# Twenty-eight of forty conditioning slabs move from the attentions to the feed-forward and from TensorE to VectorE

## What is computed

```python
silu_c = jax.nn.silu(c)
silu_cc = jax.nn.silu(c_ctx)
for layer in range(DEPTH):
    want_ctx = layer < DEPTH - 1
    mod = silu_c @ w_mod[layer] + b_mod[layer]      # 1024 -> 6 * 1024
    cmod = silu_cc @ w_mod[layer] + b_mod[layer]
    sh1, sc1, g1, sh2, sc2, g2 = jnp.split(mod[:, None, :], 6, axis=-1)
    ...
    hx = modulate(rms_norm(x, norm1_g[layer]), sh1, sc1)
    mx, mc = token_mixers(hx @ w_in[layer], ...)     # attentions, pooling, gates, projections
    x = x + g1 * mx
    hx = modulate(rms_norm(x, norm2_g[layer]), sh2, sc2)
    ...
    f = swiglu(h_all, ...) if layer % 2 == 0 else moe_swiglu(h_all, ...)
    ...
    x = x + g2 * fx
```

## Time and profile before

| | us |
|---|---|
| median of 3 runs | 2029.77 (2026.84 to 2030.6) |
| profiled execution | 2027.18 |
| its span, first to last instruction | 2025.4 |

### The profile page before, as it was taken

How to read it: one execution, slowest core, us unless ns; L and a number is a source line. 1 busy time by engine, 2 the same in 40 slices (tenths; PEclk the granted TensorE clock), 3 DMA queues, 4 the chain that set the end, 5 groups by cost and what they waited for, 6 DMA issues and landing times.

```text
span 2025.4 us, 48866 instructions
## 1 busy us (share of the span) xinstructions
PE 1977.5 (98%) x22688; PEld 1419.6 (70%) x22689; DVE 474.4 (23%) x974; ACT 458.3 (23%) x765; POOL 425.0 (21%) x145
## 2 busy tenths in 40 slices
PE   5999999999999999999999999999999999999997
PEld 3885788878888888876997566666666666666664
DVE  3246223220010101346543002111111102111112
ACT  4236522233212223436443000000000000000001
POOL 2400334446545445401550000000000000000000
PEclk8999999999999999999999999999999999999999
DMA  8338332231232323246467999999999999999990
GB/s 328 107 149 350 107 104 100 88 145 63 104 104 83 104 94 105 93 156 261 167 230 290 388 404 390 374 392 389 409 378 374 390 406 388 376 392 389 407 379 25
DMA packets 69856, 505.56 MB, mean 250 GB/s; under 512 B 7760, under 2 KB 7888, under 8 KB 9104
## 3 DMA queue, kind: packets, MB, share of 16 engines
q1 hardware_dynamic: 69264, 500.01, 64.0%
q0 software_dynamic: 384, 2.36, 0.3%
HBM read 501.29 MB, written 1.05 MB: 248 GB/s over the span
## 4 chain that ended last, share of the span: by engine, by line
PE 88%; POOL 3%; issue 3%; DMA 2%; ACT 1%; DVE 1%; SPq 0%; POOLq 0%; ACTq 0%; DVEq 0%
PE bank L1265 29%; PE bank L1277 14%; PE bank L811 12%; PE bank L812 12%; PE bank L813 12%; POOL w_lo L499 3%; DMA slab<-in_w_in 2%; PE bank L846 1%; PE turned L1040 1%; PE pv_bank L1058 1%; PE bank L1016 1%; DMA slab<-in_w_mod 1%; ACT H_NEW L1525 1%; PE bank L1251 0%; PE bank L1279 0%
## 5 line engine op out<-in xcount | busy, mean ns | idle before, releaser
L1265 PE MATMUL bank<-moe_slab,HE 128*32 128x256 f32 x10752 | 596.3, 379 | 1.3 <-DVE GT L2216 1.3
L1265 PEld LDWEIGHTS bank<-moe_slab,HE 128*32 128x32 f32 x10752 | 346.4, 110 | 231.4 <-DVE GT L2216 1.8
L499 POOL TENSOR_TENSOR w_lo<-slab,w_hi 128x2048 fp32r<-128x2048 f32 (+2 forms) x88 | 362.3, 4119 | 573.9 <-ACT w_hi L1484 573.8
L811 PE MATMUL bank<-H_HI,w_hi 128*128 128x512 f32 (+1 forms) x880 | 321.0, 365 | 4.7 <-POOL H_LO L724 3.6
L812 PE MATMUL bank<-H_LO,w_hi 128*128 128x512 f32 (+1 forms) x880 | 318.2, 362 | 0.0
L813 PE MATMUL bank<-H_HI,w_lo 128*128 128x512 f32 (+1 forms) x880 | 318.1, 361 | 0.0
L1277 PE MATMUL bank<-moe_slab,GE 128*32 128x256 f32 x4032 | 299.8, 379 | 0.0
L1279 PE MATMUL bank<-moe_slab,GE 128*32 128x256 f32 x1344 | 299.1, 379 | 0.0
L1277 PEld LDWEIGHTS bank<-moe_slab,GE 128*32 128x32 f32 x4032 | 165.8, 110 | 115.4
L1484 ACT ACTIVATE w_hi<-slab 128x2048 fp32r<-128x2048 f32 (+1 forms) x88 | 165.7, 1888 | 152.9 <-PE bank L813 145.5
L773 POOL TENSOR_TENSOR OUT<-OUT,RINVF 128x256 f32<-128x256 f32 x2 | 1.6, 814 | 946.4 <-DVE RINVF L2337 946.4
(11 more groups left out here) (229 smaller groups left out, 2032.6 us busy)
## 6 DMA issues: line engine op xcount, KB each, us to landing
moe_slab<-in_moe_up SPq DMA_DIRECT2D x224, 1024.0 KB, 7.4
moe_slab<-in_moe_w SPq DMA_DIRECT2D x112, 1024.0 KB, 7.2
slab<-in_w_in SPq DMA_DIRECT2D x38, 1024.0 KB, 4.9
slab<-in_ffn_w SPq DMA_DIRECT2D x30, 1024.0 KB, 4.8
slab<-in_w_mod SPq DMA_DIRECT2D x20, 1024.0 KB, 7.7
side_slab<-in_w_mod SPq DMA_DIRECT2D x20, 1024.0 KB, 9.1
start_slab<-in_w_mod SPq DMA_DIRECT2D x8, 1024.0 KB, 17.4
slab<-in_w_proj SPq DMA_DIRECT2D x8, 1024.0 KB, 4.9
```

What stands on the lines that cost most here:

```text
L499: engine.tensor_tensor(lo, raw, hi.bitcast(F32), ALU.subtract).then_inc(done, 1)
L811: mm(out, lhs[0], rhs[0], start=start, stop=False)
L1265: ins = mm(outs[t // 2][32 * b:32 * b + 32, 256 * (t % 2):256 * (t % 2) + 256], rows[t], w[:, 256 * b:256 * b + 256], start=first and t != ...
```

## The change

Units 10 to 23, 28 slabs, are no longer matmuls. Groups 0 to 4 (layer 0 without its last gate) stay with TensorE; six units and three turned groups run beside layer 0's attentions, in the first, third and fifth run of three steps, and none beside layer 1's.

The other seven groups come from `w_mod_rows`: the same weights transposed on the host, so that an output column lies on a partition and its 1024 weights along it. A row slab is 1 MB and holds two chunks of 128 columns. During layer 0's feed-forward VectorE multiplies each chunk by the conditioning row, which stands in every partition (COND_ROW, 1 MB, Silu on ScalarE), and sums it in the same instruction into its column of `MOD`. That is 80 instructions (48 for the 12 slabs that need both streams, 32 for the 16 that need one), placed by `mod_rows` after the HID multiplies and, in the first two parts, after each residual. Three more instructions add the biases.

SP loads COND_ROW once layer 0's second norm is through, and the row slabs into two buffers at fixed places of the ring's order (`ROW_LOADS`); from the third on each waits for the sums of the slab two before. The buffers lie on places that held BIAS, TMP and others, so layer 1's BIAS is loaded later, ahead of the slab `("in", 1, 2)`.

The diff without its context and its smaller edits (semaphores, the same conditions on the other engines):

```diff
-MOD_FIRST = (4, 16)
+MOD_FIRST = 4
 def mod_beside(layer, s):
-    return None if s % 3 == 2 else MOD_FIRST[layer] + 2 * (s // 3) + s % 3
+    q, i = divmod(s, 3)
+    return MOD_FIRST + q + i if layer == 0 and q % 2 == 0 and i < 2 else None
 def turned_beside(layer, s):
-    return MOD_FIRST[layer] // 2 + s // 3 if s % 3 == 2 else None
-OUT_OF_RING = [mod_beside(_l, _s) for _l in range(DEPTH) for _s in range(len(attention_steps(_l))) if _s % 3 == 1]
+    q, i = divmod(s, 3)
+    return (MOD_FIRST + q) // 2 if layer == 0 and q % 2 == 0 and i == 2 else None
+OUT_OF_RING = [mod_beside(0, _s) for _s in range(len(attention_steps(0))) if _s % 3 == 1 and mod_beside(0, _s)]
+MOD_GROUPS = 5
+ROW_SLABS = [(part, i) for part in range(MOD_GROUPS, 12) for i in range(4)]
+ROW_STREAMS = [2 if part <= 7 else 1 for part, _ in ROW_SLABS]
+def row_sums(r):
+    return 2 * sum(ROW_STREAMS[:r])
+ROW_LOADS = {4: 2, 7: 1, 9: 1, 11: 1, 13: 1, 14: 1, 15: 1, 16: 1, 17: 1, 19: 1, 21: 1, 23: 1, 25: 2, 26: 2, 27: 2,
+             28: 2, 29: 1, 30: 3, 32: 3}
+assert sum(ROW_LOADS.values()) == len(ROW_SLABS)
...
+        COND_ROW = at("COND_ROW", 164, [P, 2, D])
+        row_slab = [at(f"row_slab{i}", kb, [P, 2, D]) for i, kb in enumerate((172, 180))]
+        ROW_OUT = at("ROW_OUT", 148, [P, 2, D])
...
+            ffn_at = SLABS["w1", 0, 0]
+            row_at = iter(range(len(ROW_SLABS)))
+            def row_loads(n):
+                if n == 4:
+                    sp.wait_ge(h_lo_ready[0, 2], DC)
+                    sp.dma_start(COND_ROW[:].rearrange("p a n -> p (a n)"), a["cond_row"]).then_inc(cond_row_in, 16)
+                for _ in range(ROW_LOADS.get(n, 0)):
+                    r = next(row_at)
+                    if r >= 2:
+                        sp.wait_ge(rows_made, row_sums(r - 1))
+                    sp.dma_start(row_slab[r % 2][:].rearrange("p a n -> p (a n)"), a["w_mod_rows"][r])\
+                        .then_inc(row_in[r % 2], 16)
...
+                if order[n] == ("in", 1, 2):
+                    sp.wait_ge(rows_made, row_sums(len(ROW_SLABS)))
                     sp.dma_start(BIAS[:].rearrange("p a h n -> p (a h n)"), a["rel_bias"][1]).then_inc(bias_in[1], 16)
                 load_slab(n, order[n])
+                if n >= ffn_at:
+                    row_loads(n - ffn_at)
                 if order[n][0] == "mod" and order[n][1] % 2 == 0:
...
-                for i in OUT_OF_RING:
-                    if (i >= MOD_FIRST[1]) == layer:
+                if layer == 0:
+                    for i in OUT_OF_RING:
                         wait_mod(act, i)
...
+                        if before is None:
+                            act.wait_ge(cond_row_in, 16)
+                            af(COND_ROW[:], COND_ROW[:], ACT.Silu).then_inc(cond_row_ready, 1)
...
-                wait_taken(dve, ("turned_mod", 6 * layer + (1 if w == 1 else 4)))
                 part = 1 if w == 1 else 4
+                if 6 * layer + part < MOD_GROUPS:
+                    wait_taken(dve, ("turned_mod", 6 * layer + part))
+                else:
+                    dve.wait_ge(row_parts_made, 2 if w == 1 else 3)
+                streams = 1 if (layer, w) == (1, 2) else 2
                 lo = VEC_COLS[f"g{w}", layer][0]
...
+            row_of = iter([(r, m) for r in range(len(ROW_SLABS)) for m in range(2)])
+            def mod_rows(n):
+                for _ in range(n):
+                    r, m = next(row_of, (None, None))
+                    if r is None:
+                        return
+                    group, i = ROW_SLABS[r]
+                    layer, part = divmod(group, 6)
+                    streams = ROW_STREAMS[r]
+                    if m == 0:
+                        dve.wait_ge(row_in[r % 2], 16 * (r // 2 + 1))
+                    w = row_slab[r % 2][:, m, :]
+                    for n in range(streams):
+                        col = (part * DC + 2 * i + m) * 2 + n
+                        k = row_sums(r) + m * streams + n
+                        if k >= 2:
+                            dve.wait_ge(rows_made, k - 1)
+                        v.scalar_tensor_tensor(ROW_OUT[:, k % 2, :], w, 1.0, COND_ROW[:, n, :], ALU.mult, ALU.mult,
+                                               accum_out=MOD[layer][:, col:col + 1]).then_inc(rows_made, 1)
+                    if m == 0:
+                        continue
+                    if (group, i) in ((5, 3), (7, 3), (11, 3)):
+                        dve.wait_ge(rows_made, row_sums(r + 1))
+                        first = {5: 5, 7: 0, 11: 2}[group]
+                        chunks = DC * (part + 1 - first)
+                        made = MOD[layer][:, 16 * first:16 * (part + 1)].rearrange("p (c s) -> p c s", s=2)[:, :, 0:streams]
+                        lo = VEC_COLS["bmod", layer][0] + DC * first
+                        b = VEC[:, lo:lo + chunks].unsqueeze(2).to_broadcast([P, chunks, streams])
+                        v.tensor_tensor(made, made, b, ALU.add).then_inc(row_parts_made, 1)
             def feed_forward():
                 q = 0
+                dve.wait_ge(cond_row_ready, 1)
                 for part, n in enumerate(PART_CHUNKS):
                     for s in range(n // 2):
                         for m in range(2):
@@ -2121,7 +2209,17 @@
                             v.tensor_tensor(HID[:, q % 4, :], SILU[:, m, :], acc(k3)[:], ALU.mult)\
                                 .then_inc(freed(k3), 1)
                             q += 1
-                    residuals(0, 5, [("down", part, c // 2, c % 2) for c in range(DC)], (1, 1) if part == 2 else None)
+                            if m == 1 or part == 2:
+                                mod_rows(2 if m == 1 and part < 2 else 2 + 2 * m)
+                    if part == 0:
+                        dve.wait_ge(row_parts_made, 1)
+                    keys = [("down", part, c // 2, c % 2) for c in range(DC)]
+                    if part == 2:
+                        residuals(0, 5, keys, (1, 1))
+                        continue
+                    for c, key in enumerate(keys):
+                        residual(0, 5, key, c)
+                        mod_rows(1 + part)
...
-    a["w_mod"] = np.concatenate([slabs(w) for w in w_mod])
+    a["w_mod"] = np.concatenate([slabs(w) for w in w_mod])[:4 * MOD_GROUPS]
+    rows = np.concatenate([w.T for w in w_mod]).reshape(-1, 2, P, D).transpose(0, 2, 1, 3)
+    a["w_mod_rows"] = np.ascontiguousarray(rows[4 * MOD_GROUPS:]).reshape(-1, P, SLAB)
+    a["cond_row"] = np.ascontiguousarray(np.broadcast_to(
+        np.concatenate([c[0], c_ctx]).reshape(1, 2 * D), (P, 2 * D)))
```

More of the change, by code:

```diff
@@ L175, in schedule @@
         scores(1)
-        mod(mod_beside(layer, 0))
+        if layer == 0:
+            mod(mod_beside(layer, 0))
         for n in range(steps):
@@ L180, in schedule @@
                 mod(mod_beside(layer, n))
-            elif n:
+            if turned_beside(layer, n) is not None:
                 turned_mod(turned_beside(layer, n))
@@ L419, in build @@
         cond_ready, cond_zeroed = sem("cond_ready"), sem("cond_zeroed")
+        cond_row_in, cond_row_ready = sem("cond_row_in"), sem("cond_row_ready")
+        row_in = [sem(f"row_in{i}") for i in range(2)]
+        rows_made, row_parts_made = sem("rows_made"), sem("row_parts_made")
         first_pair_made = sem("first_pair_made")
@@ L614, in side_load @@
                 n = OUT_OF_RING.index(i)
-                layer = int(i >= MOD_FIRST[1])
-                if i < MOD_FIRST[layer] + 4:
-                    wait_full(sp, ("in", layer, ("u", 1)))
+                if n < 2:
+                    wait_full(sp, ("in", 0, ("u", 1)))
                 else:
@@ L636, in _ @@
                     sp.dma_start(POOL[:].rearrange("p a g n -> p (a g n)"), a["pool_mat"]).then_inc(pool_in[1], 16)
+                if order[n] == ("in", 1, 2):
+                    sp.wait_ge(rows_made, row_sums(len(ROW_SLABS)))
                     sp.dma_start(BIAS[:].rearrange("p a h n -> p (a h n)"), a["rel_bias"][1]).then_inc(bias_in[1], 16)
                 load_slab(n, order[n])
+                if n >= ffn_at:
+                    row_loads(n - ffn_at)
                 if order[n][0] == "mod" and order[n][1] % 2 == 0:
                     i = order[n][1] // 2
-                    first = MOD_FIRST[i >= MOD_FIRST[1]]
-                    if i == first + 2:
+                    if i == MOD_FIRST + 2:
                         side_load(i - 1)
                         side_load(i + 1)
-                    elif i > first + 2 and i + 1 in OUT_OF_RING:
+                    elif i > MOD_FIRST + 2 and i + 1 in OUT_OF_RING:
                         side_load(i + 1)
@@ L1865, in scale @@
             def scale(layer, w):
-                wait_taken(dve, ("turned_mod", 6 * layer + (1 if w == 1 else 4)))
                 part = 1 if w == 1 else 4
+                if 6 * layer + part < MOD_GROUPS:
[3 more added lines that the diff above has]
```

(11 more changed lines are left out.)

## The result

| | before | after |
|---|---|---|
| median | 2028.70 us (2026.84 to 2030.60, 4 runs) | 2011.89 us (2010.97 to 2013.31, 4 runs) |
| profiled execution, its span | 2027.18, 2025.4 | 2013.31, 2011.4 |
| VectorE busy | 474 us | 646.0 us |

A forecast was written before the change was run, and what follows sets the result against it. TensorE, 88% of the last-ending chain, was taken as the bound: 10.5 (layer 0) + 12.3 (layer 1) - 1.2 (start) - 0.5 (stalls) = 21.1 us off 2029.77, about 2009 us; range 2002 to 2021, its own range 2003 to 2014 (65%).

The forecast's parts named there:

- Removed work, 29.8 us forecast: Both layers' attentions: TensorE loses units and turned groups worth 12.8 us in layer 0, 17.0 in layer 1; ceiling 29.8.
- Layer 0, 10.5 forecast: Layer 0's attentions: three runs without units, bounded by ScalarE's queue, take 9.8 us each, gaining 3.5 each, 10.5 in all.
- Layer 1, 12.3 forecast: Layer 1's attentions: 17.0 us removed, less 2.8 for turns waiting behind maxima and 1.9 for a worthless first unit.
- rival (d): Layer 1's attentions: new gaps let TensorE's clock fall to 1.2 GHz, gain gone, 2030 us; 4% together with other things.
- The sums, 1.4 us forecast: Feed-forward on VectorE: each of 80 sums takes 1.4 us, 112 us in all, off the path if queue and GpSimd allow.
- rival (c): Feed-forward: sums run at half rate, 2.3 us each, delaying TensorE; 2035 us, deciding from about 2.2 us a sum; 8%.
- COND_ROW, 1.2 us forecast: Feed-forward start: ScalarE's wait for the conditioning row and its Silu delay w1's second slab, stalling TensorE 1.2 us.
- Late multiplies, 0.5 us forecast: Feed-forward's third part: sums ahead of a pair's second multiply end within 1 us of its due time; 0.5 us of stalls.

The follow-up runs named there:

- experiment 3: Changed kernel with row slabs from the thirteenth on issued one ring load earlier: median 2003.91 us, 0.9878 of the kernel before.
- experiment 6: Changed kernel without the relative-bias additions in branch B of both layers' attentions (wrong result): layer 0's attentions 76.28 us, layer 1's 44.83.
- experiment 4: Changed kernel with each sum made a reduction over the row slab alone, one SBUF operand (wrong result): feed-forward 443.16 us, total not read.
- experiment 2: Changed kernel with COND_ROW's wait and Silu moved behind the high part of w1's second slab: median 2009.12 us, 0.9908 of the kernel before.

## Why the prediction was right, and where its terms were off

**Removed work, 29.8 us forecast, 28.3 measured.** From layer 0's first scores to its first gate matmul TensorE's busy time fell from 85.18 to 73.19 us, by 12.0 where I took 12.8. (The stretches of the first table differ by 12.8, but the one before holds 0.6 us more of the pooling.) In layer 1 it fell from 55.92 to 39.66 us at full clock (experiment 3), by 16.3 where I took 17.0.

**Layer 0, 10.5 forecast, 9.2 measured; the reason was another, and that the size came near is in part luck.** I expected ScalarE's queue to bound every run without units, and 3.5 us of gain from each. From the last turn of one run to the last of the next, the three without units took 9.43, 10.36 and 8.53 us instead of 13.32, 13.31 and 11.14: they gained 3.9, 3.0 and 2.6. What keeps them from closing is not a full queue but single waits ahead of turns, 0.23, 1.17, 0.14 and 1.25 us, all ended by VectorE's scaled tile; the 0.57 us for a copy at the end stood before too. Of the 1.17, experiment 6 shows 0.9 to be the bias of branch B in the chain scores, maxima, scaling. Behind the 1.25 stands a chain too, maxima, four exponentials of ScalarE, scaling. The step should have read for layer 0 what it read for layer 1: who ends last ahead of each turn.

**Layer 1, 12.3 forecast, 9.2 measured.** At full clock it is 58.54 - 46.70 = 11.8 us, so the term's mechanism held, with terms that were each off a little: A's steps nearly closed, B's two gaps were 1.03 and 2.09 us where I took 1.0 each, and the first unit was worth nothing (the gap of 1.77 us at the start holds it). What failed is the step that dismissed the clock: rival (d) had "no row has it fall with gaps this short between such work", and asked only whether it would stay low through the stage. (Its price was wrong too: 36 us of work at half the clock would cost 36 us, not the gain of 21.) The clock fell for some 3 us at a time, worth 2.66 us here and, in the gates and experts' gathering behind, up to 2.0 more; the kernel before loses 1.5 us in that last stage as well, so the balance there is 0.5 us.

**The sums, 1.4 us forecast.** Alone one takes 1.22 us, 1.15 from start to start; in the mean 2.22, by waiting for GpSimd. That mean is the very figure from which rival (c) was to decide, and the feed-forward lost 2.8 us to the sums, not 27: a sum that waits leaves GpSimd at work. The rival's half rate is refuted by the shortest and the median sum, 1.207 and 1.220 us, and with it the Trainium skill's rule on scalar_tensor_tensor with two fp32 operands in SBUF (Vector Engine (DVE) Microarchitecture Reference, Points that are easy to get wrong): no halved rate, with an accumulator and without. Its other rule, that the second instruction waits for the whole of the first (SBUF — State Buffer, Who interferes with whom), the trace agrees with to 0.15 us in the pair shown above, and experiment 4 shows the condition: two SBUF operands.

**COND_ROW, 1.2 us forecast, 0.6 to 0.7 of wait and 0.9 in the stretch measured (experiment 2).** Transfer (4.9 us), Silu (1.92) and high part (1.90) took what was worked out. Less the 8.6 us by which the stage starts earlier, the low part ended 0.25 us before and TensorE wanted it 0.3 us after the times I gave.

**Late multiplies, 0.5 us forecast, 2.0 to 2.8 measured.** Place and chain were right, the size not: I took the last part's sums to "end within 1 us of when it is due", and the last pair's multiply came 2.8 us later than in experiment 3 (776.17 against 773.36). The cause is the two groups of three in `ROW_LOADS`, whose first slab is wanted when it is issued or before; I had followed issues and landings alone, and with sums of 2.3 us behind GpSimd the lag grows.

**From profile to profile** the 7.1 us that lack are: 1.3 layer 0, 0.5 and 2.7 layer 1 and its clock, 1.5 feed-forward, 0.5 behind, 0.8 ahead of the first scores and -0.2 from there to w1. The 0.8 us is no effect of the change: 136.6 to 140.2 us stood there in kernels with the same code.

## What to carry to other kernels

Before you take work out of a full TensorE queue, list what ends last ahead of each instruction that stays: here it was a chain through VectorE, once with ScalarE in it, and how far such gaps closed, not the size of the engines' queues, set the gain. A transfer's lateness and a lock between engines can each be harmless and stall together; here either remedy was enough, and moving a load one place earlier is the cheap one. Where gaps of 1 to 2 us open in TensorE's work, look at the clock behind them as well: here its falls cost up to 4.6 us in two stages, about as much as the waiting. Matmuls that nobody reads cost nothing where they fit in, though that they keep the clock up is not shown. Edits worth under 3 us must be judged by their rows, since medians move by more with the clock.

## What the runs showed of the hardware

- A scalar_tensor_tensor over 128x1024 fp32 from two SBUF tiles with its sum takes 1.22 us, and 0.08 us to read the accumulator, hidden in the next; a reduction of one such tile takes 1.21.
- Behind a low part of GpSimd (4.6 us) the same sum took 5.62 us, and a low part with a sum running 5.29; with one SBUF operand neither is held up (at most 1.22 and 4.77).
- The granted clock falls to 0.50 for 3 to 4 us at a time, each worth 0.7 to 1.6 us of TensorE's time in the stretches named; to the experts, a double one cost up to 2.0 us more than a single one. The same instructions with the same gaps showed it in some kernels' profiles and not in others'.
- Times of one kernel spread over 5 to 6 us: in steps of some 2.5 us in one (2006.95, 2006.99, 2009.12, 2011.65, 2011.73), without steps in another (2005.02, 2007.17, 2009.26, 2009.87, 2011.33).
